# Output projection in rounded upper and lower parts, channel norm's gain and bias on turned rows, and a new order of work on four engines

## The reference

```python
att = combine_branches(branches).reshape(B, T, D_ATT).astype(x.dtype)
...
conv = jax.nn.silu(layernorm(causal_dwconv(cext, conv_w, conv_b), ln_g, ln_b))
...
x = x + gt1 * (jnp.concatenate([att, conv], axis=-1) @ w_out)
h2 = rmsnorm(x, g_n2) * (1 + sc2) + sh2
x = x + gt2 * hierarchical_moe(h2.reshape(B * T, D), ...)
```

## Time and profile before

| What | Value |
|---|---|
| median of 3 runs | 2499.24 us (2499.19 to 2499.28) |
| the profiled execution | 2497.23 us |
| its span, first to last instruction | 2495.7 us |
| mean granted TensorE clock | 0.921 |
| PE, DVE, ACT, POOL busy | 85%, 66%, 44%, 26% of the span |
| the stage's instructions | about 1039 to 1446 us of the span |
| zero rows | 3 DMAs of 5632.0 KB each |

### The profile page before, as it was taken

The page is one execution under the profiler, slowest core; times in us unless marked ns, Lnnn a source line. Parts: engine busy times, 40 slices in busy tenths (PEclk is TensorE's granted clock), DMA queues, the critical chain, the costliest instruction groups (busy, mean ns, idle before and its releaser), DMA issues. The chain is left out here.

```text
span 2495.7 us, 36927 instructions
## 1 busy us (share of the span) xinstructions
PE 2130.3 (85%) x11790; PEld 1630.7 (65%) x11791; DVE 1643.2 (66%) x3121; ACT 1099.7 (44%) x1979; POOL 648.3 (26%) x536
## 2 busy tenths in 40 slices
PE   6999999996999983469999849999999999999800
PEld 3788888884777762235555538888888888888700
DVE  2668888895666675248888547856544666448766
ACT  2311111125777880012222228765645666558632
POOL 1025444420111113036666410000000000000066
PEclk8999999998999995689999869999999999999955
DMA  8855555556574455677333168958565878569787
GB/s 269 279 183 186 187 206 201 195 181 231 174 235 137 148 166 185 220 279 275 126 128 127 53 236 296 397 210 309 206 230 183 337 267 306 212 256 343 280 296 252
DMA packets 220144, 560.76 MB, mean 225 GB/s; under 512 B 26685, under 2 KB 40341, under 8 KB 218904
## 3 DMA queue, kind: packets, MB, share of 16 engines
q1 hardware_dynamic: 179708, 439.45, 50.2%
q0 software_dynamic: 26016, 79.49, 9.0%
q10 hardware_dynamic: 14340, 40.78, 4.4%
HBM read 461.18 MB, written 171.04 MB: 253 GB/s over the span
## 5 line engine op out<-in xcount | busy, mean ns | idle before, releaser
L586 DVE SCALAR_TENSOR_TENSOR ARENA<-ARENA,TAPW 128x512 f32<-128x512 f32 (+3 forms) x493 | 293.4, 680 | 0.0
L1832 PE MATMUL OP<-WO,MT 128*128 128x512 f32 x544 | 257.7, 635 | 0.0
L412 POOL TENSOR_TENSOR MS<-SSQ,K 128x1 f32<-128x1 f32 x17 | 168.6, 9916 | 291.1 <-ACT H L455 291.1
L2094 DVE TENSOR_TENSOR GE<-SE,BE 128x256 f32<-128x256 f32 x98 | 36.9, 418 | 273.0 <-PE BE L2136 270.7
L1832 PEld LDWEIGHTS OP<-WO,MT 128*128 128x128 f32 x544 | 110.7, 207 | 135.5 <-issue 135.5
L705 PE MATMUL PJ<-WIN_H,HTH 128*128 128x512 f32 x680 | 172.0, 395 | 14.9 <-ACT HTH L461 11.7
L1012 ACT ACTIVATE PR<-SBX,NM 128x256 f32<-128x256 f32 (+1 forms) x384 | 171.9, 455 | 1.4 <-PE TB L1099 0.8
L709 PE MATMUL PJ<-WIN_H,HTL 128*128 128x512 f32 x680 | 169.1, 391 | 0.0
L1992 POOL DMA_INDIRECT XG<-h_rows,IDX x50 | 50.2, 1005 | 454.8 <-PE XP L2125 438.4
L713 PE MATMUL PJ<-WIN_L,HTH 128*128 128x512 f32 x680 | 168.0, 389 | 0.0
L487 ACT ACTIVATE ARENA<-PJ 128x512 f32<-128x512 f32 x51 | 30.5, 600 | 288.7 <-PE PJ L713 288.7
(11 more groups left out here) (298 smaller groups left out, 4593.8 us busy)
## 6 DMA issues: line engine op xcount, KB each, us to landing
W1E<-in_w_expert_gate SPq DMA_DIRECT2D x64, 1024.0 KB, 6.3
W3E<-in_w_expert_up SPq DMA_DIRECT2D x64, 1024.0 KB
W2E<-in_w_expert_down SPq DMA_DIRECT2D x64, 1024.0 KB, 11.6
expert_rows<-YE ACTq DMA_DIRECT2D x49, 512.0 KB, 5.8
expert_rows<-NOROWS POOLq DMA_DIRECT2D x3, 5632.0 KB
WAD<-in_w_ada SPq DMA_DIRECT2D x16, 1024.0 KB, 5.3
X<-in_x_prompt SPq DMA_DIRECT2D x31, 512.0 KB
QN<-q_rows SPq DMA_DIRECT2D x48, 256.0 KB, 3.1
```

Source lines behind the costliest of these rows:

```text
L412: pool.tensor_tensor(MS[:], SSQ[:], const("eps"), ALU.add).then_inc(ms_ready, 1)
L586: ins = nc.vector.scalar_tensor_tensor(out=out, in0=src, scalar=tap, in1=out, op0=ALU.mult, op1=ALU.add)
L1832: mm = nc.tensor.matmul(OP[:, n * 512:(n + 1) * 512], MT[:, k], WO[:, k, n * 512:(n + 1) * 512], start=k == 0, stop=k == KD - 1)
L2094: nc.vector.tensor_tensor(G[:, cols], S[:, cols], BP[:, cols], ALU.mult).then_inc(g_ready, 1)
```

## The change

The output projection no longer multiplies in fp32. WO is split once into WOH, its upper part rounded to the type F32R, and WOL, the rest. Each tile's turned MIX is split likewise into MTH and MTL. `project` sums three products: MTH x WOH, MTL x WOH, MTH x WOL, first for the attention half (k 0 to 3), then for the convolution half: 48 matmuls for 16. The upper parts come from ACT, the lower parts from DVE.

The channel norm's gain and bias move from rows to turned rows, where a channel is a partition. ACT applies them as scale and bias of its activations on TPS, four for the tanh and four for the linear value, 128x128 each; the passes L1566 and L1568 on POOL go. `conv_norm` writes the normalised value to MIX directly.

The rounds of all four engines are rearranged. The zero rows are issued in rounds 3 to 13, three blocks each.

```diff
-        WO = sb("WO", [P, KD, D])
+        WO, WOH, WOL = sb("WO", [P, KD, D]), sb("WO_H", [P, KD, D], F32R), sb("WO_L", [P, KD, D], F32R)
...
-                sp.dma_start(WO[:], t["w_out"][0].rearrange("(k p) n -> p k n", p=P)).then_inc(weights_in, 16)
+                for k in range(4):
+                    sp.dma_start(WO[:, 2 * k:2 * k + 2], t["w_out"][0].rearrange("(k p) n -> p k n", p=P)[:, 2 * k:2 * k + 2]).then_inc(wo_in[k], 16)
...
# GpSimd: normalise loses two passes, the round is rearranged
-                    pool.wait_ge(y_norm, i * 2 + 1)
-                    pool.tensor_tensor(Y[:], Y[:], LNG[:], ALU.mult).then_inc(y_norm, 1)
-                    pool.wait_ge(y_norm, i * 2 + 2)
-                    pool.tensor_tensor(Y[:], Y[:], LNB[:], ALU.add).then_inc(y_ready, 1)
...
-                    if there(i + 1, TILES - 1):
-                        normalise(i + 1)
                     if there(i - 1):
                         scale(i - 1)
...
+                    if there(i + 1, TILES - 1):
+                        normalise(i + 1)
                     if there(i - 3):
                         place(i - 3, rows_of(i - 3))
-                    if isinstance(i, int) and 0 <= i < 3:
+                    if not isinstance(i, int):
...
+                        first = pool.snap(i * (3 * P) + (NEXP - 3 * 3) * P)
+                        pool.sem_inc(placing, 1)
+                        pool.dma_start(dr["y"][ds(first, 3 * P)].rearrange("(b p) d -> p b d", p=P),
+                                       NOROWS[:, None, :].to_broadcast([P, 3, D])).then_inc(norows_out, 16)
...
# ScalarE
+                    for c in range(KC):
+                        nc.scalar.activation(TH[:, c], TPS[:, HA + c], ACT.Tanh, scale=LNH[:, 0, c:c + 1], bias=LNH[:, 1, c:c + 1])
+                        ins = nc.scalar.activation(YT[:, c], TPS[:, HA + c], ACT.Identity, scale=LN[:, 0, c:c + 1], bias=LN[:, 1, c:c + 1])
+                    ins.then_inc(th_ready, 1)
...
+                    act.wait_ge(wo_in[k // 2], 16)
+                    nc.scalar.activation(WOH[:, k], WO[:, k], ACT.Copy, scale=1.0 if k < HA else 0.5).then_inc(w_hi_ready, 1)
...
                 def round_(i):
+                        take_h2(i - 1)
+                        take_att(i + 1)
+                        take_conv(i + 1)
+                        branch_weights(i + 2)
+                        squares(i, rows_of(i))
+                        route_exps(i - 1)
+                        take_swish(i + 1)
+                    if isinstance(i, int) and i == -1:
+                        for k in range(KD):
+                            upper(k)
...
# VectorE
+                    nc.vector.tensor_tensor(MTL[:, 0:HA], TPS[:, 0:HA], MTH[:, 0:HA], ALU.subtract).then_inc(att_lo, 1)
...
+                    stt(WOL[:, k], WO[:, k], 1.0 if k < HA else 0.5, WOH[:, k], ALU.mult, ALU.subtract).then_inc(w_lo_ready, 1)
...
                 def round_(i):
                         gated(i - 1, rows_of(i - 1), which_of(i - 1))
+                        att_rest(i)
+                        branches(i + 1)
+                        weigh(i - 3)
                         take_logits(i - 2)
+                        route(i - 2)
+                        swish(i)
                         rank(i - 3, rows_of(i - 3))
+                        choose(i - 2)
+                        conv_rest(i)
+                    if isinstance(i, int) and i == 0:
+                        for k in range(KD):
+                            lower(k)
                         norm(i - 1, rows_of(i - 1), which_of(i - 1))
+                        branch_shares(i + 1)
+                        moments(i + 1)
+                        attended(i + 1)
+                        conv_norm(i + 1)
...
# TensorE, project
-                            mm = nc.tensor.matmul(OP[:, n * 512:(n + 1) * 512], MT[:, k], WO[:, k, n * 512:(n + 1) * 512], start=k == 0, stop=k == KD - 1)
+                    for ks, hi, lo in ((range(HA), att_hi, att_lo), (range(HA, KD), conv_hi, conv_lo)):
+                        pe.wait_ge(hi, i + 1)
+                        products(MTH, WOH, ks, start=ks[0] == 0)
+                        pe.wait_ge(lo, i + 1)
+                        products(MTL, WOH, ks)
+                        mm = products(MTH, WOL, ks, stop=ks[0] == HA)
```

More of the change, by code:

```diff
@@ L1505, in _ @@
                 sp.dma_start(G2[:], t["g_norm2"].to_broadcast([P, D])).then_inc(mods_in, 16)
-                sp.dma_start(LNG[:], t["ln_g"].to_broadcast([P, DCONV])).then_inc(mods_in, 16)
-                sp.dma_start(LNB[:], t["ln_b"].to_broadcast([P, DCONV])).then_inc(mods_in, 16)
+                with nc.allow_non_contiguous_dma(reason="a channel of the norm's gain and bias to each partition"):
+                    sp.dma_start(LN[:, 0], t["ln_g"].rearrange("o (c p) -> p (o c)", p=P)).then_inc(mods_in, 16)
+                    sp.dma_start(LN[:, 1], t["ln_b"].rearrange("o (c p) -> p (o c)", p=P)).then_inc(mods_in, 16)
                 sp.dma_start(BR[:, 0:GROUPS], t["b_router_group"].to_broadcast([P, GROUPS])).then_inc(mods_in, 16)
@@ L1649, in round_ @@
                 def round_(i):
-                    if there(i + 1, TILES - 1):
-                        branch_weights(i + 1)
-                    if there(i - 1):
-                        squares(i - 1, rows_of(i - 1))
-                    if there(i + 1, TILES - 1):
-                        swish(i + 1)
-                    if there(i - 2):
-                        route_exps(i - 2)
                     if there(i - 1):
@@ L1668, in stt, with branches @@
                     return nc.vector.scalar_tensor_tensor(out=out, in0=in0, scalar=scalar, in1=in1, op0=op0, op1=op1)
-                def mix(i):
+                def branches(i):
                     dve.wait_ge(br_in, i * 32 + 32)
@@ L1755, in choose, with weigh @@
                     nc.vector.tensor_tensor(A[:], OH[:, 0], OH[:, 1], ALU.add).then_inc(picked, 1)
+                def weigh(i):
                     dve.wait_ge(gap_exp, i + 1)
@@ L1784, in _ @@
                 dve.wait_ge(preset, 3)
+                nc.vector.tensor_scalar(LNH[:], LN[:], 0.5, None, ALU.mult).then_inc(lnh_ready, 1)
                 def round_(i):
@@ L1819, in turn_mix @@
                     else:
-                        pe.wait_ge(mix_ready, i + 1)
+                        pe.wait_ge(y_norm, i + 1)
                         pe.wait_ge(att_ready, i + 1)
+                        if not (isinstance(i, int) and i == 0):
+                            pe.wait_ge(att_lo, i)
+                            pe.wait_ge(th_ready, i)
+                    if dec:
+                        pe.wait_ge(att_lo, i)
+                        pe.wait_ge(th_ready, i)
                     for k in range(KD):
@@ L1826, in project, with products @@
                 def project(i):
-                    pe.wait_ge(mt_ready, i + 1)
                     if not (isinstance(i, int) and i == 0):
                         pe.wait_ge(x2_half, i)
-                    for n in range(D // 512):
-                        for k in range(KD):
-                            mm = nc.tensor.matmul(OP[:, n * 512:(n + 1) * 512], MT[:, k], WO[:, k, n * 512:(n + 1) * 512], start=k == 0, stop=k == KD - 1)
+                    first = isinstance(i, int) and i == 0
+                    def products(x, w, ks, start=False, stop=False):
+                        for n in range(D // 512):
+                            for k in ks:
+                                mm = nc.tensor.matmul(OP[:, n * 512:(n + 1) * 512], x[:, k], w[:, k, n * 512:(n + 1) * 512],
+                                                      start=start and k == ks[0], stop=stop and k == ks[-1])
+                        return mm
+                    for ks, hi, lo in ((range(HA), att_hi, att_lo), (range(HA, KD), conv_hi, conv_lo)):
+                        pe.wait_ge(hi, i + 1)
+                        if first:
+                            pe.wait_ge(w_hi_ready, ks[-1] + 1)
+                        products(MTH, WOH, ks, start=ks[0] == 0)
+                        pe.wait_ge(lo, i + 1)
+                        products(MTL, WOH, ks)
+                        if first:
+                            pe.wait_ge(w_lo_ready, ks[-1] + 1)
+                        mm = products(MTH, WOL, ks, stop=ks[0] == HA)
                     mm.then_inc(proj_done, 1)
```

99 lines of the change are left out of this document (64 added, 35 removed).

## The result

The changed kernel takes **2516.38 us** (median of 4 runs, 2515.40 to 2518.31), the kernel before 2499.22 on the same chip: a ratio of 1.0072, 95% interval 1.0054 to 1.0089. It is slower, by 17 us; 2497 was forecast, with a range to 2515. The profiled execution took 2516.78 us with a span of 2514.1.

A forecast was written before the change was run, and what follows sets the result against it. The stage was to go from TensorE-bound to a GpSimd and VectorE loop of 21.4 us a round. First projection +2.3, intervals 0 to 3 -13.4, 3 to 15 +9.2, end 0: -1.9, about 2497 us, range 2485 to 2515.

The forecast's parts named there:

- a loop of GpSimd and VectorE that contains `place`: Projection and routing stage: GpSimd and VectorE hand to each other in five steps, 21.4 us a round; chance 0.38.
- Rivals C: Loop rounds: zero rows' issue costs little and the addition falls into VectorE's load wait, about 20.5 us a round, 2487 us; 0.24.
- D: Projections: TensorE's waiting drops its clock to 1.2 GHz, 27 us a round, 2560 us; chance 0.04.
- Eight matmuls: Projection on rounded operands: eight matmuls take 1.81 us at the full clock, 0.227 each.
- first gating product: Start of the stage: the first projection ends at 1089.6, 2.3 us later than before.
- tiles 0 to 3: First three intervals, free of zero rows, TensorE nearly the bound: 54 us against 67.4.
- Step 5 of the loop: GpSimd from `place` to the next addition: 5.5 us plus 1.1 for issuing three blocks of zero rows, 6.6 us.
- Steps 2 and 4: VectorE from comparison to end of `norm`, 5.8 us; share product through GpSimd's variance and power between attention sums, 4.15 us.
- tiles 3 to 15: Loop intervals of the stage: 21.0 + 10 x 21.4 + 19.8 = 254.8 us against 245.6, +9.2.
- rival B: Loop rounds: GpSimd's addition gets in before VectorE's 128x24 branch subtraction, which waits 2.34 us; 22.9 a round, 2512 us; 0.30.
- The tail: End of the stage: the last tile's addition stands behind a `place`, some 1 us longer.
- "TensorE is the bound there, but VectorE stands only 15% behind": Stage's middle before the change: of 245 us TensorE is busy 238.5, VectorE 202.5.

The follow-up runs named there:

- fp32_again: Changed kernel with only the products undone: 16 fp32 matmuls a tile on unrounded operands, roundings, differences and orders kept; 2521.3 us.
- zero_early: Changed kernel with the zero rows issued as before, 11 blocks in each of rounds 0 to 2, none in the loop; 2523.5 us.
- zero_spread: Kernel before with only the zero rows moved into the loop, three blocks in each of rounds 3 to 13; 2490.9 us.
- store_first: Changed kernel, but SyncE issues the 512 KB h2 store before the next tile's load instead of right behind it; 2506.4 us.
- slot_late: Changed kernel, but GpSimd waits for the slot DMAs only behind its next addition, and the loop begins one round later; 2486.3 us.
- place_first: Changed kernel, but in GpSimd's round place(i-3) stands before normalise(i+1); 2568.0 us.
- slot_late_parts_early: slot_late with GpSimd's wait for the slot DMAs behind scale and the load split in three, columns and statistics issued earlier; 2486.4 us.
- split_alone: Kernel before with the split products alone; gain and bias on GpSimd, zero rows and all other orders as before; 2505.4 us.
- ports_clear: slot_late_parts_early with two moves on VectorE: branches(i+1) before att_rest(i), branch_shares(i+1) before norm(i-1); 2480.8 us.
- small_load: Changed kernel, but the loop's load brings only 16 of 512 columns of each branch; 2472.1 us, not to be compared.
- best_fp32: The fastest kernel (2447.6 us, additions to X2 and of SHIFT on VectorE) with the split products undone, 16 fp32 matmuls a tile; 2488.5 us.

## Why the prediction was wrong

- **The kind of bound was right.** The stage is bound by a loop of GpSimd and VectorE that contains `place`. fp32_again shows it best: the slower products change no round. Rivals C (20.5 us a round) and D (whole projections at the 1.2 GHz level) did not take place; the clock fell to 0.84 in the mean, so TensorE worked 19 us a round instead of 17.7 and waited 2.1 us for `conv_norm` instead of 3 to 5.
- **Products and start: right.** Eight matmuls in 1.86 us for 1.81; first gating product +2.9 for +2.3; tiles 0 to 3 in 55.1 for 54, and zero_early and zero_spread show that the zero rows are the reason. (They go with eleven loop rounds, not ten; no term depends on it.)
- **Step 5 of the loop, `place` to the next addition, is the term that failed**: 6.6 us in the sum, 9.96 in the round shown (1258.82 to 1268.78). It carried the old slot wait of 2.14 us over, though that wait depends on what else is on the DMA engines, and the same prediction moved the load's issue next to it: 0.24 us behind the attention sum, and RS, after which `place` begins, between those sums. Both rows were there. The wait became 5.9; store_first takes 512 KB away and gets back 1.7 us of it (1.4 expected), and slot_late, which moves the wait, gets back 30 us of time. The Trainium skill, "DMA: Bandwidth & Descriptors", section "Queues, rings and completion order", says that a DMA's semaphore is written only after every earlier write of that DMA engine, across its queues. The runs fit this, since bulk of SyncE's queue delays GpSimd's DMAs, but they do not single it out: GpSimd went on 2.4 and 2.6 us after the engines ran empty in the two rounds shown, and before they did in place_first. By what rule the engines delay the slot DMAs stays open.
- **Steps 2 and 4 were too large** by 1.8 and 0.5 us (3.97 and 3.69 in the round shown): as the addition came late, most of the routing was over. So 21.4 became 22.5 in the round shown and 22.8 in the mean; tiles 3 to 15 took 269.1 us for 254.8, which is most of the error. That rival B's 2512 us and 22.9 us a round lie close is chance.
- **Rival B did not take place here.** With the addition that late the subtraction of the branches was long done; a 128x2 copy stood still instead (2.15 us at 1246.60). Its stall came as soon as the addition was early (2.81 us in slot_late_parts_early). The Trainium skill, "SBUF — State Buffer", section "Who interferes with whom", says that the order of issue decides who stands still, not the shape. The runs agree in part: which operation is hit followed the order in each kernel, whatever its size, but those of 2.81 and 3.27 us had begun before GpSimd's addition and stood still all the same.
- **The tail, forecast at about +1, was +5.1.** By the traces 2.2 us of it lie in GpSimd's wait for the last `norm` (3.67 us, 1.45 before) and 2.5 in the slot wait behind it (3.87, 1.36 before). No run tested them.
- **"TensorE is the bound there, but VectorE stands only 15% behind" was read too kindly.** VectorE's waits were 1.8 us a round, split_alone could use 0.3 of them, and in zero_spread the round stayed the same with TensorE busy 15 us less. So the loop of VectorE and GpSimd was about as long as TensorE's work already before the change, and faster products alone had little to gain.

## What to carry to other kernels

Before moving a wait for a small DMA, list what is issued within a few microseconds of it on any queue: by these runs it lands 2 to 4 us later when bulk travels with it, so put the wait where nothing long stands behind it. An engine's room is at most its waiting time in the round, not one minus its busy share; how much of it can be used only a run tells. And where GpSimd's long elementwise passes meet many small VectorE operations, give the pass to VectorE: 1.23 us of its own work replaced 3 us of standing still, and the two moved additions alone brought the changed kernel from 17 us above the one before to 23 below it.

## What the runs showed of the hardware

- A VectorE operation on one element in each partition lasted 3.27 us in ports_clear (0.16 in the changed kernel); it began 0.85 us before GpSimd's addition, as GpSimd began to issue a DMA, and ended with the addition.
- GpSimd stands still too: its 128x1 operation at 1256.12 of the changed kernel, begun 0.15 us after VectorE's 128x1536 product, took 1.65 us (0.19 in the kernel before) and ended with the product.
- The issue of an indirect DMA took 2.50 us instead of 1.06 at one place of place_first, as VectorE ran its 128x1536 product beside it; the cause was not tested.
- Two indirect DMAs of 128 numbers each let GpSimd wait 2.1 us when the engines were free (kernel before), 4.1 (store_first), 4.6 (small_load) and 5.9 us (changed kernel) with bulk issued beside them.
- TensorE's granted clock held 1.00 for 110 us and then 0.92 with the same work in best_fp32: 18.8 against 20.4 us a round of fp32 products. How far the split pays thus hangs on the clock; why it changed is not known.
